# An FFN in two phases: up tiles in pairs by seven half products, squares kept in DRAM

## The chip, the cores and the metric

The kernel runs on one core of one Trainium2 chip. The metric is the device time of one execution in microseconds. Engines are named as the profile names them: PE is TensorE, DVE VectorE, ACT ScalarE, POOL GpSimd, SP SyncE, whose DMA queue moves weights here.

## The reference

Two blocks of layers over 1,024 tokens of 1,024 features in float32. The change touches one step of the second block, its feed-forward network (FFN), with `w_up` of 1024 x 4096 and `w_down` of 4096 x 1024; `h` is the running 1024 x 1024 state.

```python
def second_block(x, p, g_mix, w_in, ..., g_mlp, w_up, w_down, g_ple, w_ple_gate, w_ple_proj, g_final):
    ...
        h = h + jnp.concatenate([conv_out, attn], axis=-1) @ w_out[i]
        m = rmsnorm(h, g_mlp[i])
        h = h + jnp.square(jax.nn.relu(m @ w_up[i])) @ w_down[i]
        gate = jax.nn.sigmoid(rmsnorm(h, g_ple[i]) @ w_ple_gate[i])
        h = h + gate * (p[i] @ w_ple_proj[i])
    return rmsnorm(h, g_final)
```

## The kernel before

Everything is transposed: features lie on partitions, tokens along the row, so `H` is eight tiles of 128x1024. Each float32 operand is split in a high part and a low rest (`w_hi`, `w_lo`; `raw_hi`, `raw_lo`), and a product is three: high by high, low by high, high by low. One PE instruction is 128x128 weights by 128x512 tokens.

The FFN's 4,096 hidden features are eight blocks of four tiles. An **up tile** is 128 hidden features by 1,024 tokens: 8 feature tiles x 3 x 2 token halves = 48 products (`up`, L1459). The root of the norm is applied after the product, so DVE evicts with one instruction that does max(0, x) times the root (`up_tile`, L2973), ACT squares it (L2176), and ACT and DVE split the square in high and low part.

A **down slab** is 512 hidden features by 256 output features. Its product is made by seven products in the place of eight (a 2x2 scheme over tile pairs and token halves, order `SEVEN`), with four sums of weights (`weight_sums`, DVE, L3010 to L3015) and four of squares (`ffn_u_sums`, DVE, L2980 to L2993). Seven times 2 x 3 = 42 products (`down`, L1485). The result of each is added to `H` or to `SHARED` by DVE (`down_added`, L3032). All seven go through the four banks 4 to 7 of PSUM; up tiles use 0 to 3. The last block is not done so: `last_down` (L1507), four slabs of 48 products.

The order is written out by hand: block b's first two up tiles, the four down slabs of block b-1, block b's other two up tiles. Squares of one block stand in SBUF until the down slabs that follow have read them. SP fetches weight slabs of 512 KB in one loop, each when POOL has split the slab two before it (`s_w_ready`, L614). POOL makes both parts of every weight, the high by a cast (`entry_hi`, L707) and the low by a subtraction (L711), 128x256 at a time, into a ring of eight entries that PE's products free again.

## Time and profile before

| | us |
|---|---|
| median of 3 timed runs | 2646.43 (2645.07 to 2648.64) |
| span of the profiled execution | 2643.2 |
| first product of the FFN's up tiles to last product of `last_down` | 1876.5 to 2536.6 |
| PE, DVE, POOL, ACT busy | 2572.9, 1599.2, 1140.9, 1001.6 |

The profiled execution is told by its span, from its first to its last instruction; timed runs are a little longer. In its rows a matmul's duration is longer than the distance to the next one, since they are pipelined. An instruction of DVE, ACT or POOL that had to wait for a port shows it as duration, not as idle time before it.

### The profile page before, as it was taken

To read this page: it belongs to the slowest core of one execution; us is meant where nothing else is said; L and a number is where in the kernel's file an instruction comes from. 1 tells how busy PE (TensorE), PEld (TensorE's weight loads), DVE (VectorE), ACT (ScalarE), POOL (GpSimd) and SP (SyncE) were. 2 spreads that over 40 slices of the span, in tenths; PEclk is the share of its full clock that TensorE was granted. 3 is DMA by queue.
4 is the path that set the end of the run, shared out by engine and by line. 5 is a ranking of instruction groups with operands and counts; after the bars stand their busy time and mean duration, and the time that the engine had idled before them with its cause. 6 is when DMAs were issued, how large, how long until landed. Compare 5 with 4: busy or idle time off the path is not lost.

```text
span 2643.2 us, 33209 instructions
## 1 busy us (share of the span) xinstructions
PE 2572.9 (97%) x12880; PEld 2055.9 (78%) x12880; DVE 1599.2 (61%) x1936; ACT 1001.6 (38%) x1434; POOL 1140.9 (43%) x1422
## 2 busy tenths in 40 slices
PE   8999999999999999999999999999999999999998
PEld 6877878687787787877776777767888888888886
DVE  6636663777647648557776455564455565555556
ACT  3527881436405315225365445563201111111132
POOL 4633344532432432432442222214565557655653
PEclk9999999999999999999999999999999999999999
DMA  3110002212112112111230010003111111111312
GB/s 139 48 51 27 24 25 90 86 59 100 52 55 73 58 49 71 66 59 66 90 112 24 25 33 25 33 17 104 56 49 48 48 56 56 54 43 49 120 47 80
DMA packets 44822, 156.36 MB, mean 59 GB/s; under 512 B 4928, under 2 KB 5312, under 8 KB 44672
## 3 DMA queue, kind: packets, MB, share of 16 engines
q1 hardware_dynamic: 31392, 110.11, 12.8%
q10 hardware_dynamic: 13280, 44.17, 4.6%
q8 instruction: 103, 1.69, 0.3%
q14 instruction: 47, 0.39, 0.0%
HBM read 141.55 MB, written 12.71 MB: 58 GB/s over the span
## 4 chain that ended last, share of the span: by engine, by line
PE 85%; DVE 8%; ACT 4%; issue 2%; POOL 1%; ACTq 0%; DVEq 0%; POOLq 0%
PE PS L784 38%; PE PS L1459 13%; PE PS L1485 10%; PE PS L1114 4%; PE PS L1021 3%; PE PS L1507 2%; PE PS L1347 1%; PE PS L920 1%; PE PS L1330 1%; PE PS L1147 1%; PE PS L1157 1%; PE PS L1151 1%; PE PS L934 1%; PE PS L1370 1%; DVE mla_neg_max L2397 1%
## 5 line engine op out<-in xcount | busy, mean ns | idle before, releaser
L637 POOL CAST w_hi<-w_stage 128x1024 fp32r<-128x1024 f32 x130 | 145.0, 1115 | 1048.4 <-PE PS L784 758.2
L640 POOL TENSOR_TENSOR w_lo<-w_stage,w_hi 128x256 fp32r<-128x256 f32 x520 | 492.9, 979 | 10.4
L784 PE MATMUL PS<-XH,w_hi 128*128 128x512 f32 x1216 | 386.7, 399 | 9.0 <-ACT ssd_z L1899 3.3
L784 PE MATMUL PS<-XL,w_hi 128*128 128x512 f32 x1216 | 375.9, 390 | 0.0
L784 PE MATMUL PS<-XH,w_lo 128*128 128x512 f32 x1216 | 375.4, 390 | 0.0
L784 PEld LDWEIGHTS PS<-XH,w_hi 128*128 128x128 f32 x1216 | 221.5, 188 | 65.4 <-issue 12.9
L784 PEld LDWEIGHTS PS<-XH,w_lo 128*128 128x128 f32 x1216 | 228.3, 188 | 48.7
L784 PEld LDWEIGHTS PS<-XL,w_hi 128*128 128x128 f32 x1216 | 228.3, 188 | 48.6
L711 POOL TENSOR_TENSOR w_lo<-w_stage,w_hi 128x256 fp32r<-128x256 f32 x260 | 220.1, 853 | 0.0
L707 POOL CAST w_hi<-w_stage 128x256 fp32r<-128x256 f32 x260 | 125.7, 486 | 185.6 <-PE PS L1459 108.2
L1459 PE MATMUL PS<-raw_hi,w_hi 128*128 128x512 f32 x512 | 158.2, 390 | 0.0
L1459 PE MATMUL PS<-raw_hi,w_lo 128*128 128x512 f32 x512 | 157.8, 389 | 0.0
L1459 PE MATMUL PS<-raw_lo,w_hi 128*128 128x512 f32 x512 | 157.7, 389 | 0.0
L1485 PE MATMUL PS<-ffn_u_hi,w_hi 128*128 128x512 f32 x392 | 152.6, 389 | 0.0
L1485 PE MATMUL PS<-ffn_u_hi,w_lo 128*128 128x512 f32 x392 | 152.6, 389 | 0.0
L1485 PE MATMUL PS<-ffn_u_lo,w_hi 128*128 128x512 f32 x392 | 152.6, 389 | 0.0
L3032 DVE TENSOR_TENSOR H<-H,PS 128x512 f32<-128x512 f32 x140 | 96.1, 686 | 76.9 <-PE PS L1485 76.9
L2973 DVE SCALAR_TENSOR_TENSOR ffn_t<-PS,root 128x1024 f32<-128x1024 f32 x32 | 39.2, 1225 | 154.2 <-PE PS L1459 145.0
L2176 ACT ACTIVATE ffn_t<-ffn_t 128x1024 f32<-128x1024 f32 x32 | 34.0, 1061 | 240.1 <-DVE ffn_t L2973 240.1
L1459 PEld LDWEIGHTS PS<-raw_hi,w_hi 128*128 128x128 f32 x512 | 96.1, 188 | 20.3 <-issue 0.5
L1459 PEld LDWEIGHTS PS<-raw_lo,w_hi 128*128 128x128 f32 x512 | 96.1, 188 | 19.9
L1459 PEld LDWEIGHTS PS<-raw_hi,w_lo 128*128 128x128 f32 x512 | 96.1, 188 | 19.9
(459 smaller groups left out, 5421.5 us busy)
## 6 DMA issues: line engine op xcount, KB each, us to landing
w_stage<-w SPq DMA_DIRECT2D x202, 512.0 KB, 3.4
ssd_sum_rows<-sums_kept ACTq DMA_DIRECT2D x32, 512.0 KB, 3.7
H<-x_t ACTq DMA_DIRECT2D x8, 512.0 KB, 8.3
pj_kept<-ple_proj_tiles ACTq DMA_DIRECT2D x8, 512.0 KB, 2.6
h_kept<-H ACTq DMA_DIRECT2D x8, 512.0 KB, 3.0
H<-h_kept ACTq DMA_DIRECT2D x4, 1024.0 KB, 5.5
out_t<-out_tiles SPq DMA_DIRECT2D x16, 256.0 KB, 2.1
x_again<-x_t ACTq DMA_DIRECT2D x12, 256.0 KB, 3.1
```

Of the source, the lines that this page charges most:

```text
L637: nc.gpsimd.tensor_copy(w_hi[:, slot, :, :], w_stage[:, slot, :, :]).then_inc(s_w_hi, 1)
L640: nc.gpsimd.tensor_tensor(w_lo[:, slot, k:k + 2, :], w_stage[:, slot, k:k + 2, :], w_hi[:, slot, k:k + 2, :].bitcast(F32), ALU.subtract).t ...
L707: nc.gpsimd.tensor_copy(ring(w_hi, e), src).then_inc(s_eh.sem, 1)
L711: nc.gpsimd.tensor_tensor(ring(w_lo, e), src, ring(w_hi, e).bitcast(F32), ALU.subtract).then_inc(done, count)
L784: mm = nc.tensor.matmul(outs[:, half, :], wt[:, slot, k, :], a[:, k - first, half * HB:(half + 1) * HB], start=(k == whole[0] and wt is w_ ...
L1021: mm = nc.tensor.matmul(PS[:, 2 * (n % 2) + half, :], wt[:, n % 2, k, :], a[:, k, half_cols(half)], start=(k == 0 and wt is w_hi and a is ...
L1114: mm = nc.tensor.matmul(PS[:, half, :], wt[:, n % 2, k, :], a[:, k, half * HB:(half + 1) * HB], start=(k == 0 and wt is w_hi and a is XH), ...
L1459: mm = nc.tensor.matmul(PS[:, 2 * (c % 2) + half, :], ring(wt, e + k // 2, k % 2), a[:, k, half * HB:(half + 1) * HB], start=(k == 0 and w ...
L1485: mm = nc.tensor.matmul(PS[:, BANK[j], :], ring(wt, e + i, k), a[:, ACTS_AT[j], k, :], start=(j not in BEFORE and k == 0 and wt is w_hi an ...
L1507: mm = nc.tensor.matmul(PS[:, 4 + 2 * e + half, :], ring(wt, e0 + k // 2, k % 2), a[:, t, half * HB:(half + 1) * HB], start=(first and wt ...
L2973: v.scalar_tensor_tensor(out=FT[:, c % 2, :], in0=flat(c % 2), scalar=0.0, in1=RSQ[:, :], op0=ALU.max, op1=ALU.mult).then_inc(s_ue, 1)
L3032: v.tensor_tensor(dst, dst, src, ALU.add).then_inc(s_dr, 1)
```

## The change

The FFN is cut in two phases: all up tiles, then all down slabs.

Up tiles are taken in 16 **pairs** (hidden tiles q and q+2 of a block). Pairs 0 and 1 are made as before (`up_plain`). The other 14 are made by seven **half products** of 4 x 3 = 12 PE instructions (`up_pair`), in the order of `SEVEN`: P1, P6, P5, P7, P2, P3, P4. They need four sums of the tokens, made once and split (`token_sums`, `sums_hi`, `sums_lo`), and four sums of the pair's two weight slabs, all made by DVE (`pair_sums`, L3411 to L3416, 128x512 each). The two sets of four PSUM banks change from pair to pair. DVE puts the products together (`u2`, `u3`, `c22`, `c12`, `c21`, and `f` for max and root), a quarter of the pair at a time; ACT copies the first product out, squares the quarters, and now makes the high part of all weights of pairs and down slabs (`pair_hi`, `down_hi`); POOL is left with the low parts, 128x512 for a pair (`pair_part`).

The seven square quarters and differences of a pair (`diff`, `u_hi`, `u_lo`) go to one of five SBUF places and from there to DRAM (`u_kept`, 512 KB each, on SP's queue); pairs 14 and 15 have four. In the second phase SP loads a block's seven in four groups, 7.3 MB per block, into one of two places (`load`); down slabs now change between two sets of four banks. `last_down` reads its squares from DRAM too.

```diff
-FFN_ORDER = [("up", 0, 0), ("up", 0, 2), ("up", 0, 1), ("up", 0, 3)]
-for _b in range(1, FFN_BLOCKS):
-    FFN_ORDER += ([("up", _b, 0), ("up", _b, 2)] + [("down", _b - 1, _s) for _s in range(4)]
-                  + [("up", _b, 1), ("up", _b, 3)])
+SEVEN = [1, 6, 5, 7, 2, 3, 4]
+PAIRS, PLAIN_PAIRS, DOWN_BLOCKS = 2 * FFN_BLOCKS, 2, FFN_BLOCKS - 1
+FFN_ORDER = [("up", _p // 2, _q) for _p in range(PAIRS) for _q in (_p % 2, _p % 2 + 2)]
+FFN_ORDER += [("down", _b, _s) for _b in range(DOWN_BLOCKS) for _s in range(4)]
...
+for _n in range(N_FFN, pair_slab(PLAIN_PAIRS)):
+    _uses(_n, 4, {3: _n + 1}, 1)
+for _p in range(PLAIN_PAIRS, PAIRS):
+    _uses(pair_slab(_p), 7, {4: pair_slab(_p) + 1, 6: pair_slab(_p) + 2}, 2)
+for _n in range(pair_slab(PAIRS), N_PLE - 4):
+    _uses(_n, 7, {6: _n + 1}, 1)
...
-BANK = {1: 4, 2: 4, 6: 5, 5: 6, 3: 6, 7: 7, 4: 7}
+BANK = {1: 0, 2: 0, 6: 1, 5: 2, 3: 2, 7: 3, 4: 3}
...
+SPLIT_PAIRS = 2 * DOWN_BLOCKS
+QUADS = [[1, 3, 5, 7, 6, 2, 4] if _p < SPLIT_PAIRS else [1, 3, 8, 2] for _p in range(PAIRS)]
+U_PLACES = 8
+PLACE_ORDER = [4, 5, 6, 7, 4, 5, 6] + [_g % 5 for _g in range(len(PLACES) - 7)]
...
+        u_kept = nc.dram_tensor("u_kept", (DOWN_BLOCKS, 7, P, 2, 2, HB), F32, kind="Internal").ap()
+        u_last_kept = nc.dram_tensor("u_last_kept", (4, P, 2, 2, HB), F32, kind="Internal").ap()
...
-            with sp.Fori(1, NSLAB // 2) as i:
+            with sp.Fori(1, pair_slab(PLAIN_PAIRS) // 2) as i:
...
+            def next_slab(n):
+                sp.wait_ge(s_w_ready, 4 * (n - 1))
+                fetch(n, n % 2)
+
+            def store(j, p):
+                r, _ = place_turn(j, p)
+                s_ul.wait(sp, LOWS.index((j, p)) + 1)
+                if p < SPLIT_PAIRS:
+                    dst = u_kept[p // 2, SEVEN.index(j), :, p % 2, :, :]
+                else:
+                    dst = u_last_kept[RAW_QUAD[j], :, p % 2, :, :]
+                sp.dma_start(dst, U_PLACE[r][:, :, :].bitcast(F32)).then_inc(s_us[r].sem, 16)
...
+            def load(b, group):
+                first, last = 2 * group, min(2 * group + 2, 7)
+                if b >= 2:
+                    n = FFN_AT["down", b - 2, 3]
+                    used(USED[ENTRY[n] + last - 1])
...
+                sp.dma_start(dst.rearrange("p q i l t -> p q (i l t)").bitcast(F32),
+                             u_kept[b, first:last, :, :, :, :].rearrange("q p i l t -> p q (i l t)")).then_inc(s_ur[b % 2][group].sem, 16)
...
+            next_slab(pair_slab(PLAIN_PAIRS))
+            next_slab(pair_slab(PLAIN_PAIRS) + 1)
+            stores(0, slice(0, 7))
+            for p in range(PLAIN_PAIRS + 1, PAIRS):
+                stores(p - 2, slice(0, 2))
+                next_slab(pair_slab(p))
+                stores(p - 2, slice(2, 7))
+                next_slab(pair_slab(p) + 1)
+            p = PAIRS - 1
+            stores(p - 1, slice(0, 2))
+            next_slab(d0)
+            stored(2)
+            used(pair_use(p, 0))
+            load(0, 0)
+            stores(p - 1, slice(2, 4))
+            used(pair_use(p, 1))
+            load(0, 3)
+            next_slab(d0 + 1)
+            used(pair_use(p, 4))
+            load(0, 1)
+            used(pair_use(p, 5))
+            load(0, 2)
+            stores(p, slice(0, 2))
+            next_slab(d0 + 2)
+            stores(p, slice(2, 4))
+            used(pair_use(p, 6))
+            stored(4)
+            for group in range(4):
+                load(1, group)
+            next_slab(d0 + 3)
+            for b in range(DOWN_BLOCKS - 1):
+                next_slab(d0 + 4 * b + 4)
+                next_slab(d0 + 4 * b + 5)
...
+            def pair_part(p, i):
...
+                s_ah.wait(pool, 7 * turn + i + 1)
+                done, count = (s_w_ready, 4) if i in (4, 6) else (s_pd.sem, 1)
+                nc.gpsimd.tensor_tensor(ring(w_lo, e, 2), src, ring(w_hi, e, 2).bitcast(F32), ALU.subtract).then_inc(done, count)
...
+            def up_pair(p):
+                n, turn = pair_slab(p), p - PLAIN_PAIRS
+                e = ENTRY[n]
+                for i, j in enumerate(SEVEN):
+                    if i in (4, 6):
+                        pe.wait_ge(s_w_ready, 4 * (n + 1 + (i == 6)))
+                    else:
+                        s_pd.wait(pe, 5 * turn + i + 1 - (i > 4))
...
+                    if j == 2:
+                        s_p1.wait(pe, turn + 1)
+                    elif j in BEFORE:
+                        pe.wait_ge(s_ue, up_read({3: "c22", 4: "u3"}[j], p))
+                    elif turn >= 2:
+                        pe.wait_ge(s_ue, up_read({1: "f11", 6: "u2", 5: "c12", 7: "c21"}[j], p - 2))
...
+                    for k in range(4):
+                        for wt, hl in ((w_hi, 0), (w_hi, 1), (w_lo, 0)):
...
+                    elif d >= 2:
+                        pe.wait_ge(s_dr, product_turn((d - 2) // 4, (d - 2) % 4, AFTER_LAST[j]))
...
+            def first_copied(p):
...
+                nc.scalar.activation(U2[:, :], PS[:, 4 * (p % 2) + BANK[1], :], ACT.Copy).then_inc(s_p1.sem, 1)
...
+            def pair_hi(p, i):
+                j, n = SEVEN[i], pair_slab(p)
+                e, turn = ENTRY[n] + 2 * i, p - PLAIN_PAIRS
+                used(USED[e + 1 - RING])
...
+                nc.scalar.activation(ring(w_hi, e, 2), src, ACT.Copy).then_inc(s_ah.sem, 1)
...
+            for p in range(PLAIN_PAIRS, PAIRS):
+                if p > PLAIN_PAIRS:
+                    square_quad(p - 1, "f21")
+                u_hi(QUADS[p - 1][2], p - 1)
+                first_copied(p)
+                pair_hi(p, 4)
+                for j in QUADS[p - 1][3:]:
+                    u_hi(j, p - 1)
+                pair_hi(p, 5)
+                pair_hi(p, 6)
+                if p + 1 < PAIRS:
+                    pair_hi(p + 1, 0)
+                else:
+                    down_hi(0, 0)
+                    down_hi(0, 1)
+                square_quad(p, "f22")
+                square_quad(p, "f11")
+                u_hi(1, p)
+                u_hi(3, p)
+                if p + 1 < PAIRS:
+                    pair_hi(p + 1, 1)
+                    pair_hi(p + 1, 2)
+                else:
+                    for i in range(2, 6):
+                        down_hi(0, i)
+                square_quad(p, "f12")
+                if p + 1 < PAIRS:
+                    pair_hi(p + 1, 3)
...
+            def u2(p):
+                s_p1.wait(dve, p - PLAIN_PAIRS + 1)
+                used(pair_use(p, 1))
+                v.tensor_tensor(U2[:, :], U2[:, :], up_bank(p, 6), ALU.add).then_inc(s_ue, 1)
+
+            def u3(p):
+                used(pair_use(p, 3))
+                dve.wait_ge(s_ue, up_read("u2", p))
+                v.tensor_tensor(f_part(3), U2[:, :], up_bank(p, 7), ALU.add).then_inc(s_ue, 1)
+
+            def c22(p):
+                used(pair_use(p, 2))
+                dve.wait_ge(s_ue, up_read("u3", p))
+                v.tensor_tensor(f_part(3), f_part(3), up_bank(p, 5), ALU.add).then_inc(s_ue, 1)
...
+            def diff(j, p):
+                r, before = place_turn(j, p)
+                if before:
+                    s_us[r].wait(dve, 16 * before)
+                out = u_place(j, p, 1).bitcast(F32)
+                if j == 5:
+                    dve.wait_ge(s_fq, squared(p, "f12"))
+                    a, b_, op = f_part(8), f_part(1), ALU.subtract
...
+            def u_lo(j, p):
+                if j in (6, 7):
+                    s_tt.wait(dve, DIFFS.index(({7: 6, 6: 4}[j], p)) + 1)
+                s_uh.wait(dve, PLACES.index((j, p)) + 1)
+                src = f_part(j) if j in RAW_QUAD else u_place(j, p, 1).bitcast(F32)
...
+            def pair_sums(p):
+                n, turn = pair_slab(p), p - PLAIN_PAIRS
+                a11, a12, a21, a22 = (w_stage[:, m, 4 * h:4 * h + 4, :] for m in range(2) for h in range(2))
+                for slot in range(2):
+                    dve.wait_ge(s_w_loaded[slot], 16 * (n // 2) + 16)
+                if turn:
+                    dve.wait_ge(s_w_ready, 4 * n)
+                else:
+                    s_us[6].wait(dve, 32)
+                    s_us[7].wait(dve, 16)
+                v.tensor_tensor(WS2[:, 0, :, :], a21, a22, ALU.add).then_inc(s_ws, 1)
+                dve.wait_ge(s_ws, 3 * turn + 1)
+                v.tensor_tensor(WS2[:, 1, :, :], WS2[:, 0, :, :], a11, ALU.subtract).then_inc(s_ws, 1)
+                dve.wait_ge(s_ws, 3 * turn + 2)
+                v.tensor_tensor(WS2[:, SUM_AT[7], :, :], a11, a21, ALU.subtract).then_inc(s_w3.sem, 1)
+                v.tensor_tensor(WS2[:, 3, :, :], a12, WS2[:, 1, :, :], ALU.subtract).then_inc(s_ws, 1)
 
...
+            def u_steps(p, following):
+                u_lo(1, p)
+                u_lo(3, p)
+                if p >= PLAIN_PAIRS:
+                    c21(p)
+                    f(2, p)
+                if p >= SPLIT_PAIRS:
+                    u_lo(8, p)
+                    if following:
+                        u2(following)
+                    u_lo(2, p)
+                    return
+                diff(5, p)
+                diff(7, p)
+                diff(6, p)
+                u_lo(5, p)
+                diff(4, p)
+                if following:
+                    u2(following)
+                u_lo(7, p)
+                u_lo(2, p)
+                u_lo(6, p)
+                u_lo(4, p)
+
+            for j in (5, 6, 7, 4):
+                token_sums(j)
+            up_tile(0, 0)
+            sums_lo(6, 1)
+            up_tile(0, 1)
+            sums_lo(5, 2)
+            u_steps(0, None)
+            up_tile(1, 0)
+            pair_sums(PLAIN_PAIRS)
+            up_tile(1, 1)
+            u_steps(1, PLAIN_PAIRS)
+            for p in range(PLAIN_PAIRS, PAIRS):
+                u3(p)
+                c22(p)
+                f(3, p)
+                f(1, p)
+                if p + 1 < PAIRS:
+                    pair_sums(p + 1)
+                else:
+                    weight_sums(0, 0)
+                c12(p)
+                f(8, p)
+                u_steps(p, p + 1 if p + 1 < PAIRS else None)
+            for d in range(4 * DOWN_BLOCKS):
+                down_added(d // 4, d % 4, ((d + 1) // 4, (d + 1) % 4) if d + 1 < 4 * DOWN_BLOCKS else None)
+            for s in range(4):
...
```

SP's queue before, its weight loop (`w_stage` is the place of two weight slabs; the ISA rows are waits):

```order
L620 ISA
L614 ISA
L614 DMA w_stage_49<-w 128x1024
L614 ISA
L614 DMA w_stage_49<-w 128x1024
L620 REGISTER_ALU
L620 COMPARE_AND_BRANCH
```

SP's queue of the change, one pair of the first phase from its first weight slab on (`ffn_u_place` are the five places):

```order
L715 DMA w_stage_49<-w 128x1024
L737 DMA u_kept<-ffn_u_place3_164 128x1024
L737 DMA u_kept<-ffn_u_place4_165 128x1024
L737 DMA u_kept<-ffn_u_place1_162 128x1024
L737 DMA u_kept<-ffn_u_place0_161 128x1024
L737 DMA u_kept<-ffn_u_place2_163 128x1024
L715 DMA w_stage_49<-w 128x1024
L737 DMA u_kept<-ffn_u_place3_164 128x1024
L737 DMA u_kept<-ffn_u_place4_165 128x1024
```

Seven stores of an earlier pair now stand in the queue that had weight slabs alone, five of them between a pair's two slabs.

DVE before, the end of a block's down slabs and the splits that follow (`H` and `ffn_shared` take the down products, `ffn_t` is the square):

```order
L3032 TENSOR_TENSOR H_52<-H_52,PS 128x512 x5
L2980 TENSOR_TENSOR ffn_u_sums_159<-ffn_t_149 128x512
L2982 TENSOR_TENSOR ffn_u_lo_158<-ffn_t_149,ffn_u_hi_157 128x512
L2984 TENSOR_TENSOR ffn_u_lo_158<-ffn_u_sums_159,ffn_u_hi_157 128x512
L2989 TENSOR_TENSOR ffn_u_sums_159<-ffn_t_149 128x512
L2991 TENSOR_TENSOR ffn_u_sums_159<-ffn_u_sums_159,ffn_t_149 128x512
L2993 TENSOR_TENSOR ffn_u_sums_159<-ffn_t_149,ffn_u_sums_159 128x512
L2995 TENSOR_TENSOR ffn_u_lo_158<-ffn_t_149,ffn_u_hi_157 128x2x512
L2999 TENSOR_TENSOR ffn_u_lo_158<-ffn_u_sums_159,ffn_u_hi_157 128x2x512
```

DVE of the change, from a pair's weight sums to the first difference (`up_partial` is u2, `up_w_sums` the sums):

```order
L3411 TENSOR_TENSOR up_w_sums_155<-w_stage_49 128x512
L3413 TENSOR_TENSOR up_w_sums_155<-up_w_sums_155,w_stage_49 128x512
L3415 TENSOR_TENSOR up_w_sums_155<-w_stage_49 128x512
L3416 TENSOR_TENSOR up_w_sums_155<-w_stage_49,up_w_sums_155 128x512
L3357 TENSOR_TENSOR ffn_t_149<-up_partial_159,PS 128x512
L3371 SCALAR_TENSOR_TENSOR ffn_t_149<-ffn_t_149,root_151 128x512
L3399 TENSOR_TENSOR ffn_u_place3_164<-ffn_t_149,ffn_u_place3_164 128x512
L3399 TENSOR_TENSOR ffn_u_place4_165<-ffn_t_149,ffn_u_place4_165 128x512
L3361 TENSOR_TENSOR ffn_t_149<-up_partial_159,PS 128x512
L3371 SCALAR_TENSOR_TENSOR ffn_t_149<-ffn_t_149,root_151 128x512
L3392 TENSOR_TENSOR ffn_u_place0_161<-ffn_t_149 128x512
```

Weight sums of the next pair now stand between the parts of this pair's result, and the differences come behind them.

## Rows read from the trace of the kernel before

**Rows 1.** The page, busy us, share of span and instructions by engine.

```profile
PE 2572.9 (97%) x12880; PEld 2055.9 (78%) x12880; DVE 1599.2 (61%) x1936; ACT 1001.6 (38%) x1434; POOL 1140.9 (43%) x1422
```

**Rows 2.** Windows, two blocks of the FFN.

```profile
core 0: us, PE busy (x) PEld busy (x) DVE busy (x) ACT busy (x) POOL busy (x), PEclk, DMA share, GB/s
1943.00:2019.00 76.00, 76.00 (x337) 62.91 (x337) 46.02 (x66) 11.95 (x14) 46.26 (x80) 1.00 0.17 56
...
2396.00:2471.00 75.00, 75.00 (x333) 62.10 (x332) 39.86 (x59) 8.51 (x10) 47.11 (x83) 1.00 0.16 50
```

**Rows 3.** Up, down and last products: ns min/median/max, first and last start us.

```profile
L1459 PE MATMUL PS<-raw_hi,w_hi x512: 388/389/798, 1876.5 to 2491.8; 128*128 128x512 f32 x171
...
L1485 PE MATMUL PS<-ffn_u_hi,w_hi x392: 388/389/390, 1943.5 to 2470.5; 128*128 128x512 f32 x196
...
L1507 PE MATMUL PS<-ffn_last_u_hi,w_lo x64: 388/389/393, 2493.8 to 2536.6; 128*128 128x512 f32 x64
```

**Rows 4.** Timeline of DVE: start us, us, instruction, idle before.

```profile
2028.94 0.68 DVE L3032 TENSOR_TENSOR ffn_shared<-ffn_shared,PS 128x512 f32<-128x512 f32 x1
2029.54 0.68 DVE L3032 TENSOR_TENSOR H<-H,PS 128x512 f32<-128x512 f32 x1
...
2067.64 0.69 DVE L2991 TENSOR_TENSOR ffn_u_sums<-ffn_u_sums,ffn_t 128x512 f32<-128x512 f32 x1
2068.37 0.69 DVE L2993 TENSOR_TENSOR ffn_u_sums<-ffn_t,ffn_u_sums 128x512 f32<-128x512 f32 x1
```

**Rows 5.** Timelines of DVE and of POOL, the same two microseconds.

```profile
2063.99 1.07 DVE L2980 TENSOR_TENSOR ffn_u_sums<-ffn_t 128x512 f32<-128x512 f32 x1
2064.98 1.22 DVE L2982 TENSOR_TENSOR ffn_u_lo<-ffn_t,ffn_u_hi 128x512 fp32r<-128x512 f32 x1
2066.13 0.68 DVE L2984 TENSOR_TENSOR ffn_u_lo<-ffn_u_sums,ffn_u_hi 128x512 fp32r<-128x512 f32 x1
...
2063.77 1.88 POOL L711 TENSOR_TENSOR w_lo<-w_stage,w_hi 128x256 fp32r<-128x256 f32 x2
2066.20 0.86 POOL L707 CAST w_hi<-w_stage 128x256 fp32r<-128x256 f32 x1 [0.55 <-PE PS L1459]
```

**Rows 6.** POOL's subtractions: timeline, and groups with count, busy us, mean ns.

```profile
2029.92 0.73 POOL L711 TENSOR_TENSOR w_lo<-w_sums,w_hi 128x256 fp32r<-128x256 f32 x1
...
2034.77 0.74 POOL L711 TENSOR_TENSOR w_lo<-w_stage,w_hi 128x256 fp32r<-128x256 f32 x1
...
2074.65 1.43 POOL L711 TENSOR_TENSOR w_lo<-w_stage,w_hi 128x256 fp32r<-128x256 f32 x2
...
L654 POOL TENSOR_TENSOR mla_q_lo<-mla_q,mla_q_hi 128x1024 fp32r<-128x1024 f32 x8 | 19.0, 2378 | 78.7 <-ACT mla_q_hi L1664 78.7
```

**Rows 7.** Timeline of ACT, three casts in a row.

```profile
1902.40 0.62 ACT L2184 ACTIVATE ffn_u_hi<-ffn_t 128x512 fp32r<-128x512 f32 x1
1902.93 0.62 ACT L2186 ACTIVATE ffn_u_hi<-ffn_u_sums 128x512 fp32r<-128x512 f32 x1
1903.45 1.05 ACT L2190 ACTIVATE ffn_u_hi<-ffn_t 128x1024 fp32r<-128x1024 f32 x1
```

**Rows 8.** DMA issues (count, KB, us to landing); issue times of two loads.

```profile
ple_proj_a<-pj_kept ACTq DMA_DIRECT2D x1, 2048.0 KB, 10.3
ple_proj_b<-pj_kept ACTq DMA_DIRECT2D x1, 2048.0 KB, 15.0
...
2471.39 0.37 ACTq L2218 DMA_DIRECT2D ple_proj_a<-pj_kept  x1
2471.79 0.53 ACTq L2218 DMA_DIRECT2D ple_proj_b<-pj_kept  x1
```

**Rows 9.** Windows of 1 us behind those two issues; last column GB/s.

```profile
2471.00:2472.00 1.00, 1.00 (x6) 0.84 (x5) 0.62 (x1) 0.62 (x1) 0.73 (x3) 1.00 0.00 0
2472.00:2473.00 1.00, 1.00 (x7) 0.81 (x6) 0.60 (x2) 1.00 (x2) 1.00 (x2) 1.00 0.67 78
...
2475.00:2476.00 1.00, 1.00 (x6) 0.81 (x5) 1.00 (x2) 0.00 (x0) 0.69 (x1) 1.00 0.97 393
2476.00:2477.00 1.00, 1.00 (x6) 0.84 (x5) 1.00 (x3) 0.00 (x0) 0.15 (x1) 1.00 1.04 426
...
2482.00:2483.00 1.00, 1.00 (x6) 0.80 (x6) 0.67 (x1) 0.00 (x0) 0.71 (x2) 1.00 1.02 410
```

**Rows 10.** Windows around a gap of PE early in the kernel; PEclk is third from last.

```profile
388.85:391.20 2.35, 0.00 (x1) 0.00 (x1) 1.84 (x3) 2.12 (x4) 2.35 (x2) 1.00 0.34 136
391.20:395.10 3.90, 3.90 (x18) 3.51 (x19) 0.99 (x2) 2.39 (x5) 3.90 (x3) 0.56 0.00 0
```

**Rows 11.** DVE in the FFN by form: count, busy us, mean ns.

```profile
L3032 DVE TENSOR_TENSOR H<-H,PS 128x512 f32<-128x512 f32 x140 | 96.1, 686 | 76.9 <-PE PS L1485 76.9
...
L2982 DVE TENSOR_TENSOR ffn_u_lo<-ffn_t,ffn_u_hi 128x512 fp32r<-128x512 f32 x14 | 14.1, 1005 | 0.5 <-ACT ffn_u_hi L2184 0.5
```

665 lines of the change are left out of this document (422 added, 243 removed).

## The prediction

> **What bounds the kernel now.** First the page's list of busy time: TensorE is busy for 97% of the span and no other engine for more than 61% [rows 1]. Then the stretch that the change touches, by windows: in a whole block of the FFN TensorE is busy for all 76.00 or 75.00 us, at full clock, VectorE for some 40 to 46 and GpSimd for some 47 [rows 2]. Then the products themselves. The FFN issues 3 x (512 + 392 + 64) = 2,904 products of 128x512, the first at 1876.5 and the last at 2536.6 [rows 3], so one every 660.1 / 2,903 = 0.2274 us; their 389 ns overlap. The FFN is therefore TensorE's, without a gap, and what is gained is only what is taken from its queue, as long as nothing else becomes late. An up tile pair costs 96 products, 21.83 us; a down slab 42, 9.55 us.
>
> **What the change removes.** Fourteen of sixteen up pairs go from 96 products to 84 (seven half products of 12): 168 x 0.2274 = **-38.2 us**, a pair now 19.10 us and each of its parts P1, P6, P5, P7, P2, P3, P4 2.73 us. Down and last products keep their number. This term is certain; the question is whether the other engines can feed a pair every 19.1 us.
>
> **What a pair now asks of them.** VectorE: six instructions with a PSUM input (u2, u3, c22, f11, c12, c21) and eighteen with both inputs in SBUF (three f, four weight sums, four differences, seven low parts), all 128x512. A plain one follows the next by 0.60 us, one that needs the result before it by 0.73 [rows 4]: 24 x 0.60 plus six dependences of 0.13 is 15.2 us. GpSimd: seven subtractions of 128x512; none stands in the trace. By two of 256 columns at 0.69 each, start to start, it is 1.37, by half of one of 1024 columns 1.19 [rows 6]; I take 1.25, between them. ScalarE: some 19 instructions of 0.53 [rows 7], 10 us, with room.
>
> The two sums are not independent. In [rows 5] GpSimd's two subtractions (1.43 us when alone, [rows 6]) and two VectorE instructions that read SBUF twice (0.60 each when alone) take turns: 1.88 us for the one, 2.14 for the two others, each starting to move when the other ends. The third VectorE row there, when only a later cast competes, is back at 0.68. Instructions with a PSUM input beside the same GpSimd work (2029.54 beside 2029.92) keep their 0.68 [rows 4, 6]. So of a pair, 18 x 0.60 + 7 x 1.25 = 19.6 us share one port, already more than 19.1. The Trainium skill ("SBUF — State Buffer", section "Who interferes with whom") says that such a pair of instructions exclude each other for a whole instruction; the timeline agrees. By the mean row of L2982 alone, 1005 ns against 686 [rows 11], three such meetings would cost 1.0 us in the walk below and not 3.0, and the pair 22.0 us and not 24.0.
>
> **The ring that sets the pair.** SyncE's queue is now in this order for each pair: two stores, first weight slab, five stores, second weight slab (the second order rows of the change). Walk it from the start of the weight sums of pair p+1 (time 0), when that pair's second slab has landed:
> - VectorE: four sums, c12, f12, two low parts, c21, f21, difference 5: eleven instructions, 6.6 us plus three dependences, 7.0. GpSimd's parts 2, 3 and 4 of pair p+1 can start only after the sums and fall into this row; each blocks an SBUF instruction (f12, both low parts) for up to 1.25: 0.5 + 1.25 + 1.25 = +3.0. Difference 5 ends at 10.0.
> - ScalarE behind it: high part of u5, copy of P1, high part of weight part 5: 3 x 0.6, 11.9. GpSimd waits 0.5 for difference 4 and takes 1.25: the first slab's place is free at 13.7.
> - Only now SyncE issues the first slab of pair p+2, and behind it five stores and the second slab: seven transfers of 0.52 MB. The last low part ends at 18.5, so the second slab's issue, at 19.0, is not what is late. The first bytes move 1.0 us after an issue, and a full queue moves some 410 GB/s [rows 8, 9]: 1.28 us each. 13.7 + 0.1 + 1.0 + 7 x 1.28 + 0.2 for the last receipt = **24.0 us**, when the sums of pair p+2 can start.
>
> So a pair takes 24.0 us, against 19.10 of products and 21.83 before: the stores in front of the second slab replace TensorE as the bound. VectorE has u3, c22, f22 and f11 behind its last low part (to 21.2) and stands at the sums for 2.8 us in each pair. TensorE waits in two places, before P2 (weights) and before P3 (c22 behind u3), 1.3 and 3.5 us. Gaps of 2.35 us have the granted clock at 0.56 in the next 3.9 us [rows 10], which costs 1.7 us; in a pair that stays under the 24.0.
>
> Bounds for the pair. If GpSimd always found VectorE in a PSUM instruction or idle, the 3.5 us of blocking go: 20.5. If the queue moved at the mean pace of the two 2 MB loads issued together, which had landed 15.4 us after the first issue ([rows 8], [rows 9]; 14.2 us of transfer for eight times 0.52 MB, 1.77 each), the ring is 27.4. I take 24.0, since [rows 9] are rows of a full queue with 4 KB rows like these.
>
> **The sum of the first phase.** Four plain slabs as before, 43.7 us. Pair 1's splits then start when its second tile is out, and by the same walk pair 3's sums start at 62.6. Twelve rings follow (pairs 2 to 13 are split seven ways): 62.6 + 12 x 24.0 = 350.6. The last two pairs make four parts only; the products of pair 15 end 21.4 us after its sums: 372.0. Before, the same products took 43.7 + 14 x 21.83 = 349.3: **+22.7 us** (-19.3 at 20.5, +63.5 at 27.4). At the very start the 16 token sums (16 x 0.60 on VectorE and GpSimd's plain splits in turn with them) stand ahead of the first tile's eviction, due at 21.8: I count +1.
>
> **The seam between the phases.** On SyncE's one queue now stand, from 14.2 us after the sums of pair 15: weights (to 15.5), group 0 of block 0's squares (2.1 MB, to 20.6), two stores (23.2), group 3 (25.8), weights (27.1), group 1 (32.2), group 2 (37.3), two stores, weights, two stores (43.7), the 7.3 MB of block 1 (61.6), weights of slab 3 (63.1 landed). TensorE finishes pair 15 at 21.4, needs group 1 at 24.1 and group 2 then at 35.1: it waits 8.3 + 2.4 us. Slab 2's additions on VectorE stand behind the weight sums of slab 3, so its product 3 waits from 58.0 to 66.1: 8.1. Together **+18.8**, and two of the waits are long enough for the clock: +3.4. From there a block's 7.3 MB (17.9 us) goes in 38.2 us; the weights behind it land 13.5 us after the block's start, the adds then are at most 0.2 late: +1 in all. The two sets of four banks take no wait away, since there was none. At the slower pace of the queue the seam would cost some 12 us more; if the order were kept but nothing queued, nothing.
>
> Sum: +22.7 + 1 + 18.8 + 3.4 + 1 = **+47 us**. The span was 2643.2 us; the median of the timed runs, 2646.4, lies 3.2 above it and I keep that: 2693. The spread of the runs and a short comparison let one tell a change of about 0.2%, 5.3 us, from none.
>
> **Rivals.**
> - *TensorE stays the bound.* If the second slab is not behind the stores in effect (transfers that overlap, sums that are not waited for), a pair takes 19.1 us and the full -38.2 comes, less the seam's 18.8: 2646.4 - 38.2 + 18.8 = 2627, the side of a gain. It holds as soon as the ring is below 19.1 us; break-even is near 20.1. For it: VectorE's own 15.2 us and ScalarE's 10 fit. Against it: the seven transfers alone are 9.0 us of the ring and the chain in front of them 10.3 without any blocking.
> - *The port costs nothing.* Ring 20.5: -19.3 + 24.2 = +5, 2651, hardly to be told from no change. Against it: [rows 5].
> - *The queue is slower.* Stores and loads mixed, squares and weights in turns: ring 27.4, seam +12: +63.5 + 1 + 30.8 + 4.4 = +100, 2746. For it: the eight transfers of [rows 8] took 14.2 us, not 10.2. The Trainium skill ("DMA: Bandwidth & Descriptors", section "Where 436 GB/s comes from") puts the HBM's share of a core at some 358 GB/s; that would be 1.46 us a transfer, an estimate by that page of 25.3 for the ring. [Rows 9] show 393 to 426 for loads; no row shows a long mixture.
>
> **How the numbers follow.** Forecast (ring of 22.5 to 26) 0.64, TensorE stays the bound 0.14, port free 0.10, slower queue 0.12. Time: 2693. The forecast's own range is 2693 - 18 to 2693 + 24 plus 6 for the seam, 2675 to 2723. For eight in ten I go down to the time with a free port and up some way to the slower queue: 2645 to 2728. Faster by over 0.2%: 0.15; within: 0.09; slower: 0.76.
>
> **What would show it.** Starts of two first weight sums (L3411) one pair apart: 24 us, not 19.1 or 21.8. VectorE idle before L3411 some 2.8 us, put down to a transfer; TensorE waiting for w_lo at P2 and for VectorE's ffn_t (c22) at P3; up phase some 372 us long and the granted clock below 1 in it; GpSimd's 128x512 subtractions at a mean clearly over 1.3 us, and VectorE's low parts over 0.69. At the seam a wait of some 8 us for ffn_u_even in the first down slab and one of 8 us in the third. I am wrong if VectorE's wait before L3411 is under 0.5 us, or if the second slab lands within 4 us of its issue: then the queue was never full.

## Result and profile after

The changed kernel takes **2745.07 us** (median of four runs, 2743.59 to 2747.84) where the kernel before took 2645.75 beside it: 1.0373 times as long, 95% interval 1.0359 to 1.0388. Its profiled span is 2743.4 us against 2643.2, so the traces differ by the same 100 us. The forecast was 2693, its range 2645 to 2728: the side was right, the size was not, and the time is that of the third rival, the slower queue.

The page's list of busy time, which answers [rows 1]: TensorE does 168 products less and is busy for 94% of the span in place of 97%; VectorE has 179 us more to do, waits for the port included.

```profile
PE 2576.8 (94%) x12712; PEld 2045.9 (75%) x12712; DVE 1777.9 (65%) x2140; ACT 1156.5 (42%) x1810; POOL 1101.8 (40%) x1102
```

Windows of the FFN, with the columns of [rows 2]: one pair in the middle of the up phase, the last 200 us of that phase, the seam, the down phase without `last_down`.

```profile
2026.00:2051.00 25.00, 20.88 (x83) 16.87 (x82) 20.78 (x25) 10.79 (x19) 11.29 (x7) 0.88 0.50 190
...
2076.50:2276.00 199.50, 170.42 (x681) 135.86 (x679) 166.27 (x193) 85.12 (x152) 89.81 (x58) 0.92 0.51 183
2276.00:2324.00 48.00, 28.58 (x115) 22.50 (x114) 20.74 (x34) 11.23 (x28) 17.50 (x23) 0.83 0.92 377
2324.00:2593.00 269.00, 250.90 (x1060) 205.16 (x1061) 160.28 (x275) 67.33 (x169) 131.64 (x183) 0.96 0.54 212
```

In [rows 2] TensorE was busy for every microsecond at full clock. Now it has idle time in each window and the granted clock is 0.83 to 0.96: stretches of 3.4 to 10.2 us at the lower level (1.2 GHz), each where TensorE has stood. Its waits in the FFN: what waited, for whom, us in total, how often, the longest.

```profile
PE PS L1690 <- DVE ffn_t L3353: 48.2, 13, 4.2
PE PS L1713 <- POOL w_lo L935: 26.3, 7, 8.8
PE PS L1713 <- DMA ffn_u_even<-u_kept: 8.6, 1, 8.6
PE PS L1690 <- POOL w_lo L923: 6.3, 8, 3.8
PE PS L1690 <- DVE ffn_t L3299: 3.4, 1, 3.4
PE PS L1713 <- issue: 2.6, 1, 2.6
```

**One ring.** VectorE's timeline between the sums of two pairs, with SyncE's queue behind it:

```profile
2050.99 0.69 DVE L3411 TENSOR_TENSOR up_w_sums<-w_stage 128x512 f32<-128x512 f32 x1 [3.43 <-issue]
...
2055.36 3.48 DVE L3399 TENSOR_TENSOR ffn_u_place<-ffn_t,ffn_u_place 128x512 fp32r<-128x512 f32 x2
...
2071.68 0.68 DVE L3371 SCALAR_TENSOR_TENSOR ffn_t<-PS,root 128x512 f32<-128x512 f32 x1
2076.55 0.69 DVE L3411 TENSOR_TENSOR up_w_sums<-w_stage 128x512 f32<-128x512 f32 x1 [4.18 <-issue]
...
2063.95 0.33 SPq L715 DMA_DIRECT2D w_stage<-w  x1
2064.33 5.66 SPq L737 DMA_DIRECT2D u_kept<-ffn_u_place  x5
2070.04 0.93 SPq L715 DMA_DIRECT2D w_stage<-w  x1
```

From sums to sums 25.56 us. The first slab is issued 12.96 after the sums, the second at 19.05, behind the last store; VectorE is through with everything else at 2072.4 and stands for 4.18 us. The profile writes `issue` there, which means that it shows nothing that VectorE waited for; but by the landing times in the trace the second slab landed 6.43 us after its issue, at 2076.47, and in each of the twelve rings below the sums start 0.08 us behind that landing. Over the twelve rings from the sums of pair 3 (1950.31) to those of pair 15 the mean is 25.35. Windows of 1 us behind these issues (as [rows 9], last column GB/s):

```profile
2065.00:2066.00 1.00, 1.00 (x6) 0.84 (x5) 1.00 (x3) 1.00 (x3) 0.26 (x1) 1.00 1.21 205
2066.00:2067.00 1.00, 1.00 (x6) 0.81 (x5) 1.00 (x2) 0.18 (x1) 1.00 (x1) 1.00 0.68 209
...
2069.00:2070.00 1.00, 0.00 (x0) 0.00 (x0) 1.00 (x2) 0.00 (x0) 1.00 (x2) 1.00 1.03 422
...
2073.00:2074.00 1.00, 1.00 (x4) 0.81 (x3) 0.00 (x0) 0.97 (x3) 0.00 (x0) 0.50 0.92 254
2074.00:2075.00 1.00, 1.00 (x3) 0.72 (x3) 0.00 (x0) 0.21 (x1) 0.00 (x0) 0.50 1.01 393
2075.00:2076.00 1.00, 1.00 (x4) 0.82 (x3) 0.00 (x0) 0.00 (x0) 0.00 (x0) 0.60 0.43 160
```

While the first slab's bytes begin, the queue moves 205 to 209 GB/s for 2 us; then, with the stores, 410 to 422. It falls to 254 once more at 2073, the second slab issued 3 us before and the last two stores not yet landed, and to 160 at the end. No row tells the bytes of two transfers apart. The page's DMA issues, as [rows 8], give a slab 3.4 us from issue to landing, as a whole.

The groups that answer [rows 6] and [rows 11] (count, busy us, mean ns):

```profile
L923 POOL TENSOR_TENSOR w_lo<-up_w_sums,w_hi 128x512 fp32r<-128x512 f32 x56 | 92.4, 1659 | 134.6 <-ACT w_hi L2472 133.1
L3399 DVE TENSOR_TENSOR ffn_u_place<-ffn_t,ffn_u_place 128x512 fp32r<-128x512 f32 x50 | 70.9, 1444 | 5.1 <-ACT ffn_u_place L2438 5.1
L3399 DVE TENSOR_TENSOR ffn_u_place<-ffn_u_place 128x512 fp32r<-128x512 f32 x56 | 66.2, 1201 | 0.0
```

**The start.** Timelines of VectorE and GpSimd while pair 0 is split:

```profile
1902.87 10.10 DVE L3399 TENSOR_TENSOR ffn_u_place<-ffn_t,ffn_u_place 128x512 fp32r<-128x512 f32 x2
...
1918.23 0.69 DVE L3392 TENSOR_TENSOR ffn_u_place<-ffn_t,ffn_u_place 128x512 f32<-128x512 f32 x1 [2.66 <-DMA u_kept<-ffn_u_place]
...
1926.54 0.69 DVE L3411 TENSOR_TENSOR up_w_sums<-w_stage 128x512 f32<-128x512 f32 x1 [3.01 <-DMA u_kept<-ffn_u_place]
...
1929.20 1.22 DVE L3299 SCALAR_TENSOR_TENSOR ffn_t<-PS,root 128x1024 f32<-128x1024 f32 x1
...
1900.76 11.67 POOL L942 TENSOR_TENSOR ffn_token_sums<-ffn_token_sums_f,ffn_token_sums 128x2048 fp32r<-128x2048 f32 x2
```

Two low parts of VectorE take 10.10 us beside two 128x2048 subtractions of GpSimd; and twice VectorE waits for stores. The last row of VectorE is the eviction of pair 1's second tile. **The later blocks:** VectorE's first weight sum waits for its slab, six times, 4.4 us at the longest.

```profile
DVE w_sums L3428 <- DMA w_stage<-w: 21.9, 6, 4.4
```

**Where the 100 us are.** The FFN begins at 1874.9 (1.6 earlier than before). Up phase 1874.9 to 2276.1, 401.2 us where the same sixteen pairs took 349.3 at 21.83 each: +51.9. Seam, three gaps of TensorE of 2.56, 8.65 and 8.84: +20.05. Six gaps in the later blocks, 3.41, 2.46, 3.69, 3.57, 2.56 and 1.73: +17.4. What is left of the 101.8 us by which the FFN is longer, 12.4, is the half clock of the down phase (37.5 us of it stand at that level). 101.8 - 1.6 = 100.2.

### The profile page after: what moved, and what is told of

Same layout as the page of the kernel before. It is cut to its first block, busy times and chain, and to the rows that moved or that the text cites. A ratio compares the mean times of both kernels' runs of the same rounds, so it can differ in the third digit from the quotient of the medians.

```text
span 2743.4 us, 33505 instructions
## 1 busy us (share of the span) xinstructions
PE 2576.8 (94%) x12712; PEld 2045.9 (75%) x12712; DVE 1777.9 (65%) x2140; ACT 1156.5 (42%) x1810; POOL 1101.8 (40%) x1102
## 4 chain that ended last, share of the span: by engine, by line
PE 65%; DVE 16%; DMA 6%; ACT 6%; issue 5%; POOL 1%; SPq 0%; ACTq 0%; DVEq 0%; POOLq 0%
PE PS L984 36%; PE PS L1713 6%; DMA w_stage<-w 5%; DVE ffn_u_place L3399 4%; PE PS L1314 4%; PE PS L1221 2%; PE PS L1735 2%; PE PS L1547 1%; PE PS L1530 1%; PE PS L1347 1%; PE PS L1120 1%; PE PS L1357 1%; PE PS L1351 1%; PE PS L1134 1%; PE PS L1570 1%
## 5 line engine op out<-in xcount | busy, mean ns | idle before, releaser
L831 POOL TENSOR_TENSOR w_lo<-w_stage,w_hi 128x256 fp32r<-128x256 f32 x520 | 493.7, 980 | 10.4
L1690 PE MATMUL PS<-ffn_raw,w_hi 128*128 128x512 f32 x336 | 121.5, 447 | 53.7 <-DVE ffn_t L3353 48.2
L1713 PE MATMUL PS<-ffn_u_even,w_hi 128*128 128x512 f32 x384 | 122.3, 400 | 27.9 <-POOL w_lo L935 16.6
L923 POOL TENSOR_TENSOR w_lo<-up_w_sums,w_hi 128x512 fp32r<-128x512 f32 x56 | 92.4, 1659 | 134.6 <-ACT w_hi L2472 133.1
L1690 PE MATMUL PS<-ffn_token_sums,w_hi 128*128 128x512 f32 x448 | 141.1, 397 | 4.4 <-POOL w_lo L923 4.4
L1713 PE MATMUL PS<-ffn_u_odd,w_hi 128*128 128x512 f32 x336 | 107.2, 401 | 9.7 <-POOL w_lo L935 9.7
L1713 PEld LDWEIGHTS PS<-ffn_u_even,w_hi 128*128 128x128 f32 x384 | 73.7, 194 | 45.8 <-POOL w_lo L935 18.2
L935 POOL TENSOR_TENSOR w_lo<-w_sums,w_hi 128x256 fp32r<-128x256 f32 x112 | 82.9, 760 | 61.2 <-ACT w_hi L2484 61.1
L935 POOL TENSOR_TENSOR w_lo<-w_stage,w_hi 128x256 fp32r<-128x256 f32 x84 | 63.2, 753 | 107.1 <-ACT w_hi L2484 107.1
L1690 PEld LDWEIGHTS PS<-ffn_token_sums,w_hi 128*128 128x128 f32 x448 | 86.4, 194 | 24.2 <-POOL w_lo L923 5.6
L2917 DVE SCALAR_TENSOR_TENSOR ssd_conv<-PS,VC,ssd_conv 128x1023 f32<-128x1023 f32 (+2 forms) x72 | 92.3, 1282 | 2.6
```

Of the source, the lines that this page charges most:

```text
L831: nc.gpsimd.tensor_tensor(w_lo[:, slot, k:k + 2, :], w_stage[:, slot, k:k + 2, :], w_hi[:, slot, k:k + 2, :].bitcast(F32), ALU.subtract).t ...
L923: nc.gpsimd.tensor_tensor(ring(w_lo, e, 2), src, ring(w_hi, e, 2).bitcast(F32), ALU.subtract).then_inc(done, count)
L935: nc.gpsimd.tensor_tensor(ring(w_lo, e), src, ring(w_hi, e).bitcast(F32), ALU.subtract).then_inc(done, count)
L1690: mm = nc.tensor.matmul(PS[:, 4 * (p % 2) + BANK[j], :], ring(wt, e + 2 * i + k // 2, k % 2), up_acts(j, hl, k), start=(j not in BEFORE an ...
L1713: mm = nc.tensor.matmul(PS[:, 4 * (d % 2) + BANK[j], :], ring(wt, e + i, k), down_acts(b, j, k, hl), start=(j not in BEFORE and k == 0 and ...
L2917: ins = v.scalar_tensor_tensor(out=y[:, d:TOK], in0=src[:, 0:TOK - d], scalar=wcol(3 - d), in1=y[:, d:TOK], op0=ALU.mult, op1=ALU.add)
```

## Experiments

The prediction's account is the queue theory: SyncE's one queue sets the ring, with the port that VectorE and GpSimd share in front of it. Times below are medians with their ratio to the kernel before, measured beside it; a ring is the mean of the twelve from pair 3's to pair 15's first sum in that run's trace.

**The second slab before the last two stores.**

```diff
-                stores(p - 2, slice(2, 7))
+                stores(p - 2, slice(2, 5))
                 next_slab(pair_slab(p) + 1)
+                stores(p - 2, slice(5, 7))
```

> Of the changed kernel alone the place of the second weight slab in SyncE's queue is altered: it stands before the last two stores of a pair and not behind them. Queue theory: in the ring of 25.56 us that begins at 2050.99 the second slab was issued 19.05 us after the sums and behind it stood two stores of 1.28 us that had not moved yet; it landed at 25.3. With the two stores behind it, it is issued when its place is free (GpSimd's part P4, some 18.1 us after the sums), lands 3 to 3.4 us later, at about 22, and the ring is 22.4 instead of 25.2; VectorE's idle time before the first sum falls from 4 us to about 1. Up phase 401 - 13 x 2.8 = 365 us, time about 2709. Rival, VectorE and the port set the ring (the wait for the slab only covers something else that is late): ring stays at 25.2, time 2745. Rival, TensorE's low clock sets it: ring stays too, and the 4 us gap before P3 stays.

2725.65 us, 1.0300 (1.0282 to 1.0317); ring 23.49, up phase 378.9. VectorE's wait before the sums, 51.6 us in 13 in the changed kernel, is

```profile
DVE up_w_sums L3412 <- issue: 27.6, 13, 2.6
```

The order of the queue counts, against both rivals. But the gain is 1.86 and not 2.8 us: the slab was issued at 18.1 as expected and landed 5.2 us later, still behind a store, not 3.4.

**Short stores.** Only 16 of 128 rows of the squares of pairs 2 to 13 are stored; every block loads block 0's.

```diff
-                sp.dma_start(dst, U_PLACE[r][:, :, :].bitcast(F32)).then_inc(s_us[r].sem, 16)
+                k = 16 if 2 <= p < SPLIT_PAIRS else P
+                sp.dma_start(dst[0:k, :, :], U_PLACE[r][0:k, :, :].bitcast(F32)).then_inc(s_us[r].sem, 16)
...
```

> Leaves work out: of the squares of pairs 2 to 13 only 16 of 128 rows are stored, and every block of the down phase loads the squares of block 0. The order of the queue and every wait stay. Queue theory: the second slab is still issued only behind the last low part, some 19 us after the sums, but has nothing in front of it: it lands 3.1 to 3.4 us later, ring 22.4 to 22.7, up phase some 367 us. If instead the loads themselves were slow and the stores in front cost nothing: ring 25.2, up phase 401. If the queue were all of it and the issue no bound: ring under 21.4, VectorE's own chain.

2711.0 us (one run); ring 22.38, up phase 366.5: as expected to half a microsecond. The transfers in front of the slab cost 3.0 us of the ring; without them the issue, behind the last low part, is what is late.

**Short low parts.** GpSimd makes 64 of 512 columns.

```diff
-nc.gpsimd.tensor_tensor(ring(w_lo, e, 2), src, ring(w_hi, e, 2).bitcast(F32), ALU.subtract)
+nc.gpsimd.tensor_tensor(ring(w_lo, e, 2)[:, :, 0:16], src[:, :, 0:16], ring(w_hi, e, 2).bitcast(F32)[:, :, 0:16], ALU.subtract)
```

> Leaves work out: in the seven-way up pairs GpSimd makes only 64 of 512 columns of each low part of the weights; everything else, the waits too, stays. Port theory (the prediction's 3.0 us of blocking and the 1.25 to 1.6 us of the part itself): VectorE's low parts and differences fall from a mean of 1.2 to 1.4 us to 0.69, VectorE's chain from sums to sums from 21.4 to about 17.7, the first slab's place is free 8.3 us after the sums instead of 13.0, and with the same 12.6 us of queue behind it the ring is about 20.8; up phase some 345 us, time about 2688. Rival, the queue alone sets the ring and the port costs nothing: VectorE's means stay, only the GpSimd part itself (1.3 us) goes: ring about 23.9, up phase 384.

2698.6 us (one run); ring 21.88, up phase 357.7. VectorE's low parts in the steady pairs:

```profile
L3399 DVE TENSOR_TENSOR ffn_u_place<-ffn_u_place 128x512 fp32r<-128x512 f32 x44 | 32.0, 745 | 0.0
...
L3399 DVE TENSOR_TENSOR ffn_u_place<-ffn_t,ffn_u_place 128x512 fp32r<-128x512 f32 x35 | 22.9, 682 | 0.0
```

From 1201 and 1444 ns to 745 and 682: the blocking is GpSimd's. VectorE is through with its chain 16.3 us after the sums (mean of the twelve rings), 21.4 in the changed kernel. The ring is 3.5 us shorter, between the 4.5 of the port theory and the 1.4 of its rival; the queue from the first slab's issue to the sums still takes 12.7 us (issue 2048.32, sums 2060.99), as it did.

**Both short.** The edits of the last two runs together.

> Leaves work out, in pairs 2 to 13 both the rows of the squares stored (16 of 128, with block 0's squares loaded in every block) and 448 of 512 columns of GpSimd's low parts. The two together tell whether TensorE would carry the phase. Theory: the second slab is issued behind the last low part, some 14.8 us after the sums (18.6 less 3.8 of blocking), and lands 3.3 us later; VectorE's chain is 17.7; TensorE's 19.1 is the longest: ring 19.1 to 19.6, no gap of TensorE above 0.6 us in the steady pairs, clock full, up phase about 327 us. Rival, the two gains are the same gain: ring 21.9, as with the short low parts alone. Rival, something not counted yet (an order on ScalarE, the banks): between 20 and 21.9.

2660.3 us (one run); the rings settle at 19.04 each, up phase 324.4. A window of 219 us of it:

```profile
1980.00:2199.00 219.00, 219.00 (x968) 181.41 (x967) 173.83 (x270) 121.82 (x216) 34.47 (x82) 1.00 0.36 99
```

TensorE is busy for the whole window at full clock. So the term of -38.2 us was there to be had (a pair at 19.04, predicted 19.10), and queue and port are what keeps it away: two separate gains.

**Weights before the squares in the down phase.**

```diff
+            next_slab(d0 + 3)
             for group in range(4):
                 load(1, group)
-            next_slab(d0 + 3)
...
                 next_slab(d0 + 4 * b + 5)
+                next_slab(d0 + 4 * b + 6)
                 if b + 2 < DOWN_BLOCKS:
...
-                next_slab(d0 + 4 * b + 6)
```

> The up phase is as in the changed kernel. In the down phase the third slab of each block stands in SyncE's queue before the 7.3 MB of squares of the next but one block, and slab 3 before those of block 1. Queue theory: the gaps of TensorE in the third slab of each block (8.8 us at the seam, 3.41, 2.46, 3.69, 3.57, 2.56 and 1.73 later) were weights behind squares; they go, and the half clock behind them with most of its 12 us: 2745 - 26 - 8 = about 2711. Rival, VectorE and GpSimd are what is late there (their instructions stretched by the port): the gaps stay, 2745. Rival, the squares become late in place of the weights: gaps of 3 to 5 us before ffn_u_even and ffn_u_odd at the heads of the blocks, 2735 to 2745.

2723.17 us, 1.0289 (1.0272 to 1.0307). The wait of 8.84 at the seam is gone, the later gaps are 9.4 us in all in place of 17.4, the half clock in the down phase falls from 37.5 to 13.7 us. The gaps that are left stand one slab later than before: the fourth slab is now the one behind the loads (issued at 2423.25 where the loads began at 2414.10), as block 1's first is at the seam. 22 of the 34 us expected: the cause holds, one slab's place was overlooked.

**Short loads.** From block 2 on, 16 of 128 rows of the squares are loaded.

```diff
+                k = 16 if b >= 2 else P
-                sp.dma_start(dst.rearrange("p q i l t -> p q (i l t)").bitcast(F32),
+                sp.dma_start(dst.rearrange("p q i l t -> p q (i l t)").bitcast(F32)[0:k],
...
```

> Leaves work out: of the changed kernel alone, from block 2 of the down phase on only 16 of 128 rows of the squares are loaded; order, waits, stores and all else stay, and the seam's two blocks are loaded whole. Queue theory: the six gaps of the later blocks (17.4 us in all) were weights behind 7.3 MB of squares, and go; half clock stays only at the seam: down phase 361 - 17.4 - 5 = about 339 us, time about 2722. Rival, VectorE and GpSimd beside each other are too slow for a down slab of 9.55 us: the gaps stay, 2745.

2723.35 us (one run). TensorE's waits from the second block to the end of the phase:

```profile
PE PS L1714 <- POOL w_lo L936: 1.6, 1, 1.6
```

The gaps of the later blocks were weights behind squares; VectorE and GpSimd can feed a down slab.

**All short.** Short stores, low parts and loads.

> Leaves work out, three things at once: in pairs 2 to 13 the rows of the squares stored (16 of 128) and 448 of 512 columns of GpSimd's low parts, and from block 2 of the down phase on the rows of the squares loaded (16 of 128). If the terms are separate, the run with the first two (2660.3; ring 19.04) loses its six gaps of the later blocks, 16.8 us, and some 4 us of half clock: about 2640, under the kernel before (2645) by some 5 us. What is then still above 2645 - 38.2 = 2607 is the start of the phase (some 9 us), the seam (15.8 us of gaps) and the half clock behind both (some 8 us). If the later blocks' gaps have another cause they stay: 2660.

2641.6 us (one run), against 2640 expected: the terms are separate and add up.

**The token sums' low parts in pieces.**

```diff
+                for k in range(4):
-                nc.gpsimd.tensor_tensor(TQ[:, tq, 1, :, :], ...)
+                    part = nc.gpsimd.tensor_tensor(TQ[:, tq, 1, k, :], ...)
```

> Of the changed kernel alone the two GpSimd subtractions of 128x2048 (5.85 us each) at the start are made as eight of 128x512; the work is the same. Theory: a GpSimd instruction that reads both inputs from SBUF shuts VectorE's out until it ends; in the changed kernel VectorE's first two low parts (0.69 each when alone) took 10.10 us beside these two. In pieces VectorE gets in between: two low parts in 3 to 4 us, everything of pair 0 some 6.5 us sooner, the sums of pair 3 at 69 and not 75.4 us after the FFN's start, time about 2738. Rival, the first stores of pair 0 are late for the queue's sake or the weights set the start: 75.4 stays, 2745. Rival, the port is shared by element: the two low parts still take about 10 us.

2741.94 us, 1.0371 (1.0354 to 1.0388); the sums of pair 3 at 73.05 us after the FFN's start, not 69.

```profile
1903.50 3.47 DVE L3402 TENSOR_TENSOR ffn_u_place<-ffn_t,ffn_u_place 128x512 fp32r<-128x512 f32 x2
1906.90 3.47 DVE L3395 TENSOR_TENSOR ffn_u_place<-ffn_t 128x512 f32<-128x512 f32 x2
...
1901.39 14.78 POOL L943 TENSOR_TENSOR ffn_token_sums<-ffn_token_sums_f,ffn_token_sums 128x512 fp32r<-128x512 f32 x8
```

The two low parts take 3.47 in place of 10.10, as the port theory has it. But GpSimd is now delayed as well (14.78 in place of 11.67), and takes its turn with the next four instructions too (6.9 us for them, 2.7 before): only 2.4 us remain of the 6.5 expected.

**ScalarE's P3 and P4 first.** As the run with the second slab sooner, and

```diff
+                pair_hi(p, 5)
+                pair_hi(p, 6)
                 for j in QUADS[p - 1][3:]:
                     u_hi(j, p - 1)
-                pair_hi(p, 5)
-                pair_hi(p, 6)
```

> As the run with the second slab before the last two stores (ring 23.4 us, 2725.65), and ScalarE makes the high parts of weight parts P3 and P4 before the high parts of the squares 7, 6, 2 and 4 instead of behind them. In the run before, the second slab was issued 18.1 us after the sums, when GpSimd had ended the low part P4, and landed 5.2 us later, the two last stores still partly beside it. Queue theory: P4's low part ends some 1.7 us sooner (GpSimd goes from P2's part straight to P3's and P4's), the slab is issued at 16.4 and has landed at 21.5: ring 21.7, VectorE's idle time before the first sum gone or under 0.5, and VectorE's own chain with its blockings (21.4) now sets the ring; up phase 379 - 13 x 1.7 = 357, time about 2703. Rival, the high parts of the squares that come 1.2 us later delay VectorE's low parts: ring 23.4 or more.

2722.69 us, 1.0297 (1.0277 to 1.0317); ring 23.26 and not 21.7. GpSimd was done 16.3 us after the sums, as expected, but the slab's issue then waited behind the third store for that store's own low part (SyncE's queue, and that low part of VectorE):

```profile
2083.37 0.33 SPq L715 DMA_DIRECT2D w_stage<-w  x1
2083.74 3.90 SPq L737 DMA_DIRECT2D u_kept<-ffn_u_place  x3
2087.68 0.46 SPq L715 DMA_DIRECT2D w_stage<-w  x1
...
2085.52 1.77 DVE L3400 TENSOR_TENSOR ffn_u_place<-ffn_t,ffn_u_place 128x512 fp32r<-128x512 f32 x1
```

Sums at 2070.41, issue 17.3 later, sums again at 2093.70, 6.0 behind the issue. The rival's ring, by another way: ScalarE's high parts were in time, but GpSimd's P3 and P4 now fell on VectorE's low parts of 7 and 2 (1.19 and 1.77 us, 0.68 in the run before).

**All four orders together.**

> All four changes of order together, no work left out: second slab before the last two stores, ScalarE's P3 and P4 first, weights before the squares' loads in the down phase, token sums' low parts in pieces. By the queue theory the gains add, as they lie in different stretches: 22.3 + 22 in the rings, 6.5 at the start, 21.9 in the down phase: 2745 - 73 = about 2672, still above the kernel before (2645), since the ring of 21.7 us is VectorE's own chain and the first seam wait of 9 us stays. Rival, the gains overlap (what is taken from one stretch is waited for in the next): 2690 to 2720.

2695.53 us, 1.0189 (1.0170 to 1.0208); ring 23.36, down phase with `last_down` 335.2 in place of 361.1. 49.5 of 73 us: what is missing is the ring (12 x 1.7) and the start (pair 3's sums at 71.65).

**The second slab after two stores.** All four orders, with

```diff
-                stores(p - 2, slice(2, 7))
+                stores(p - 2, slice(2, 4))
                 next_slab(pair_slab(p) + 1)
+                stores(p - 2, slice(4, 7))
...
+                    for group in range(2):
+                        load(b + 2, group)
+                    next_slab(d0 + 4 * b + 7)
+                    for group in range(2, 4):
+                        load(b + 2, group)
```

> As the run with all four changes of order (2695.53; ring 23.3), but in SyncE's queue the second slab stands before the third of the five stores, not behind it, and in the down phase slab 3 of a block stands between the second and third load of squares, not behind all four. No work is left out. In the runs before, the second slab's issue was held by the store ahead of it, which waits for its low part (17.3 us after the sums), and it landed 6 us later behind that store. Queue theory: it is now issued when P4's low part ends, some 16.4 us after the sums, with only the first slab and two stores in front of it, and lands at 19.8 to 20.5: before VectorE's chain with its blockings ends (21.2). So ring 21.3 to 21.7, VectorE's idle time before the first sum under 0.5 us; the last 7 us of gaps in the down phase (third and fourth slab of the later blocks) go too. Time 2695 - 12 x 1.8 - 6 = about 2668. Rival, the three stores that now come later hold up the places of the next pair's squares: ring 22.5 to 23.5, with VectorE or ScalarE waiting for a store, about 2690.

2665.47 us, 1.0077 (1.0061 to 1.0094); ring 21.86. TensorE's waits in the steady pairs and the whole down phase:

```profile
PE PS L1698 <- DVE ffn_t L3361: 24.0, 12, 2.8
PE PS L1721 <- DMA ffn_u_even<-u_kept: 8.7, 1, 8.7
PE PS L1721 <- POOL w_lo L940: 1.4, 2, 0.7
```

80 us of the 100 come back by the order (and the pieces of the token sums' low parts), with no work left out. VectorE still stands 0.9 us before the sums in most pairs, but its own chain is now nearly the whole ring. The run differs from the one before it in the up phase and in the down phase at once; the ring is the up phase's part.

**VectorE makes the low parts.** As the run before, but `pair_part` runs on VectorE, in between its other instructions, the second slab stands behind one store, and ScalarE makes the high part for P4 two squares later.

```diff
-                nc.gpsimd.tensor_tensor(ring(w_lo, e, 2), src, ...)
+                v.tensor_tensor(ring(w_lo, e, 2), src, ...)
```

> As the run with the mended orders (second slab after two stores, 2665.47, ring 21.86), but VectorE makes the seven low parts of the weights of each seven-way pair, and GpSimd does nothing in these pairs; the second slab stands after the first of the five stores. No work is left out. Port theory: VectorE now has 31 instructions a pair of 0.60 to 0.61 and some 1.0 us of dependences, 19.8 us, but none is blocked; TensorE's 19.04 is nearly reached: ring 19.5 to 20.3, VectorE's low parts and differences at a mean of 0.69 and not 1.2 to 1.4, TensorE's gaps in a pair under 1 us, up phase 356 - 12 x 1.9 = 333, time about 2642, beside the kernel before at 2645 to 2646. Rival, VectorE's count of instructions is the bound and the blocking costs little: seven more of 0.6 make the ring 21.9 + 4.2 = 26, time about 2715. Rival, the high parts by ScalarE come too late for VectorE's order: between 20.5 and 22, 2650 to 2668.

2651.91 us, 1.0019 (1.0010 to 1.0028); ring 20.52, up phase 339.7. The low parts of weights and squares:

```profile
L3408 DVE TENSOR_TENSOR w_lo<-up_w_sums,w_hi 128x512 fp32r<-128x512 f32 x48 | 32.8, 683 | 0.0
L3391 DVE TENSOR_TENSOR ffn_u_place<-ffn_u_place 128x512 fp32r<-128x512 f32 x48 | 31.8, 683 | 0.0
```

Seven instructions more on the engine that set the ring make the ring 1.3 us shorter: the blocking cost more than GpSimd's help was worth. The moved slab is not what did it, as VectorE waits for it as long as before (0.8 us a ring in both); the low parts of the squares are, at 683 ns where GpSimd beside them had made them 1544 and 869. The 10 us that it missed are 0.6 us of ring, mostly a wait of 10.2 us in 13 for the slab, and a gap of TensorE of 6.82 before P6 of pair 2, for VectorE's own low part.

**No GpSimd at the start either.** The token sums' two low parts go to VectorE.

> As the run with VectorE's low parts of the weights, and the two low parts of the token sums at the start (128x2048) are VectorE's too (2.4 us each), placed where it waited 3 us each for stores. Port theory: in the changed kernel these two of 5.85 us on GpSimd shut VectorE's first square low parts out (10.10 us for two), and in pieces they still stretched the next seven VectorE instructions from some 4.5 to 10 us; with GpSimd silent the low parts and differences of pair 0 take 0.69 each, and the sums of pair 3 start some 3 us sooner than in the run before. Time some 3 us under that run, about 2639. Rival, the stores of pair 0 (whose places the weight sums take over) set the start: no change.

2646.50 us, 0.9999 (0.9990 to 1.0008), 5.4 us under that run; the 2639 expected had been reckoned from the 2642 foretold for it. Pair 3's sums at 64.95 us, 6.3 sooner than in the run before, with the ring as it was, 20.58. The stores alone do not set the start.

**Both slabs together.**

```diff
                 next_slab(pair_slab(p))
-                stores(p - 2, slice(2, 3))
                 next_slab(pair_slab(p) + 1)
-                stores(p - 2, slice(3, 7))
+                stores(p - 2, slice(2, 7))
```

> As the run without GpSimd in the pairs and token sums (2646.5; ring 20.6), but the two weight slabs of a pair stand together in SyncE's queue, no store between them. No work is left out. In the run before, VectorE stood 0.8 to 1.2 us before the first weight sum in each pair, for the second slab, which landed behind one store of 1.28 us. Queue theory: the slab lands 1.28 us sooner, VectorE's idle time goes, the ring is VectorE's own 31 instructions, 19.5 to 19.7 us, TensorE waits 0.5 us a pair; 2646.5 - 12 x 0.95 = about 2635, 0.4% under the kernel before. Rival, the stores that now come later make ScalarE's high parts (whose places they free; ScalarE waited up to 1.7 us for one) and through them VectorE's late: ring 20.5 or more, 2646 or slower.

**2637.93 us, 0.9969 (0.9958 to 0.9981)**: 0.3% below the kernel before, where 0.4% was expected. Ring 20.03, and what is left of VectorE's waits for the slab and of TensorE's for VectorE, in 235 us of the phase:

```profile
DVE up_w_sums L3413 <- issue: 3.1, 9, 0.8
...
PE PS L1673 <- DVE ffn_t L3338: 8.0, 11, 1.3
```

## Why the prediction was right in kind and wrong in size

| step | predicted | measured |
|---|---|---|
| ring | 24.0 us | 25.35 |
| start, to the sums of pair 3 | 62.6 + 1 | 75.4 |
| up phase against before | +22.7 + 1 | +51.9 |
| seam | +18.8 | +20.05 |
| later blocks | +1 | +17.4 |
| clock in the down phase | +3.4 | +12.4 |
| whole | +47 | +100.2 (profiled spans) |

The prediction fell short by 53 us: 16 of the ring, 12 of the start, 16 of the later blocks, 9 of the clock. The mechanism it put first, the second slab behind the stores, holds; four terms of its sum did not.

**What bounds the kernel before, and the removed products**: right. With queue and port out of the way a pair took 19.04 us. The rival that TensorE stays the bound is out with the ring at 25.35.

**VectorE's chain and the port**: right. The walk had the first slab's place free at 13.7 (measured 12.96), the second slab's issue at 19.0 (19.05), VectorE through at 21.2 (2072.4 is 21.4). The blocking was put at 3.0 to 3.5 us a pair; short low parts took 3.5 off the ring, of which some 0.9 is the one GpSimd instruction that stands in the chain itself (1.31 us whole, 0.4 when short). Over a whole pair VectorE's chain fell by 5.0 us: there was more blocking behind the first slab's issue than the walk had, where VectorE stood for the slab anyway. The rival of a free port is out. The Trainium skill ("SBUF — State Buffer", section "Who interferes with whom") calls the ports that the two engines share an exclusive lock, and has a VectorE instruction with two SBUF inputs contend with a GpSimd one that reads SBUF. The trace agrees: 10.10 us for two low parts beside instructions of 5.85, 3.47 beside pieces of 1.88.

**The transfers, mis-sized.** The ring's last term was 1.0 + 7 x 1.28 + 0.2 = 10.2 us after the first slab's issue, at the pace of [rows 9]; it took 12.6. By the landing times of the ring shown, the first slab took 4.02 us from its issue, where the sum has 1.0 + 1.28; the five stores behind it 7.18 for 6.4; the second slab came 1.32 behind the last of them, as priced. Over the twelve rings the first slab took 4.0 to 4.4. [rows 9] are of 2 MB loads in a full queue; the page of the kernel before has the row of a slab alone:

```profile
w_stage<-w SPq DMA_DIRECT2D x202, 512.0 KB, 3.4
```

By that row alone the sum would have had 1.1 us more for the first slab; with five stores right behind it, it took still longer. The chain in front of it was some 0.8 us shorter than walked, so it was +1.35 a ring, 16 us. Why a slab's load is slow, no run here shows; an empty queue in front of it may not be the reason, since the rate fell to 254 GB/s with the second slab behind stores too. The slower-queue rival had the total right (2746) and the ring wrong (27.4), so its hit is luck. By the figure of the Trainium skill ("DMA: Bandwidth & Descriptors", section "Where 436 GB/s comes from") the prediction's estimate for the ring was 25.3, and 25.35 came out; but not for its reason, as the stores moved at 410 to 422 GB/s.

**The start, the failed step.** "I count +1" took the 16 token sums only for the eviction of the first tile. They did no harm there (evicted 20.7 us after the start, due at 21.8). What the step left out is the other work of the same part of the change: two GpSimd subtractions of 128x2048, which shut VectorE out for 8.8 us, and `pair_sums` waiting for stores whose places it takes over. 11.8 us in all: pair 1's second tile was evicted 54.3 us after the start and not at 43.7, and from there to pair 3's sums it was 21.1 and not 18.9, for the slab as in every ring. In the run without GpSimd at the start that tile was evicted at 46.3, in the run before it at 53.7, so some 7 to 8 of the 11.8 are the two subtractions'; what the waits for stores cost was not tried by itself. The 65.0 without GpSimd, for pair 3's sums, is near the walk's 62.6 in part because the rings are shorter in that run too.

**The seam**: the two long waits are those foretold, in place and size (8.65 for `ffn_u_even`, 8.84 in the third slab). The third is not, and that the sums agree (18.8, 20.05) is in part luck: the 2.4 us before group 2 did not come, and 2.56 came before the first down product, where none was foretold. By the landing times group 0 landed at 2278.57, 24.0 us after the sums of pair 15 and not 20.6, and TensorE's first down product starts at 2278.66.

**The later blocks, the failed step that cost most after the ring.** "The weights behind it land 13.5 us after the block's start, the adds then are at most 0.2 late": that weighed 17.9 us of squares against 38.2 of products and took the third slab's sums for early enough. They were not. By the trace that slab landed 14.2 to 16.2 us after the start of a block's products, and VectorE stood ready for its sums at 11.8: landed at 13.5 it would by an estimate still have made TensorE wait some 1 us in each block (a wait of VectorE of 4.45 cost TensorE 3.69, one of 2.46 cost it 1.73), and the rest of the 17.4 is the later landing. VectorE waited up to 4.4 us for the slab, and TensorE, whose P3 of the second slab stands behind those sums, 1.7 to 3.7 in each block. (The profile names GpSimd's `w_lo` for these waits, which ended at the same time; P3 takes the bank of P5, whose addition on VectorE stands behind the sums.) Short loads and the reordered queue both took this away.

**The clock**: counted at two waits of the seam, and the four longest of the six later gaps had half clock behind them too. As the gaps were missed, so was this: +9 us. It is a remainder here, not measured by itself; with the gaps gone (the run with the slab after two stores) the half clock in the down phase fell to 10.2 us in all.

## What to carry to other kernels

When loads that are waited for share a queue with stores and bulk loads that are not, walk the queue's order in every stage, the steady ones too, and issue what is waited for first: that, with a better order on ScalarE and the token sums' pieces, gave back some 80 of 100 us here. Price a load by rows of such loads, alone or in a mixed queue, and not by a full queue's rate; here the page of the kernel before had the row. And before work is split between VectorE and GpSimd, add up both engines' instructions that read two inputs from SBUF as one engine's: here VectorE alone was faster than the two.

## What the runs showed of the hardware

- While a single 512 KB slab is loaded, the queue moves 205 to 209 GB/s for 2 us, half the rate of stores of the same size one after the other (410 to 422). The slab landed 4.0 to 4.4 us after its issue with five stores behind it, and 3.4 alone in the kernel before.
- One long GpSimd subtraction (5.85 us in the mean) holds a VectorE instruction of 0.69 us until it ends; cut in four, both engines slow each other: GpSimd's own sum went from 11.67 to 14.78 us.
- The same 128x512 subtraction takes GpSimd 1557 to 1659 ns in the mean beside VectorE and 1284 at the least, and VectorE 683 when GpSimd is silent. The Trainium skill ("GPSIMD Engine Reference", section "4.1 Engine selection") sends two-input element-wise work to VectorE, as GpSimd is about twice as slow; the trace agrees (1284 against 683), and in the last three runs it paid even with VectorE already the bound.
